# Early final norms of a two-layer encoder trunk: both whole-row passes moved into one turn, statistics one step later, the root four steps into that turn, the store issued by SP

## The chip, the core and the metric

The kernel runs on one core of a Trainium2 chip. Its engines are TensorE (PE), VectorE (DVE), ScalarE (ACT), GpSimd (POOL) and SyncE (SP); each works through its own list of instructions in order, and the lists meet only at semaphores. The metric is the device time of one execution in microseconds (us). Three executions of the kernel before took 3141.05 to 3145.18 us, median 3143.9.

## The reference, cut to what matters

Two layers. Each has a token mixer (latent attention and windowed attention) and then the block below, on 1168 tokens of width 1024 (1024 prompt frames, 128 sample frames, 16 meta tokens). All in float32.

```python
x = layer_norm(ALPHA * x + einsum('btm,md->btd', mix, w_out), ln1_g, ln1_b)
hid = silu(einsum('btd,df->btf', x, wg)) * einsum('btd,df->btf', x, wu)      # 1024 -> 2816
return layer_norm(ALPHA * x + einsum('btf,fd->btd', hid, wd), ln2_g, ln2_b)  # 2816 -> 1024
```

The change concerns the last line's `layer_norm` (the final norm) for the first 640 tokens.

## The kernel before, in words

The feed-forward block takes most of the time. Its hidden width is cut into 11 pairs of chunks (`PAIRS`), its tokens into two groups: group 0 has 640 tokens (five tiles of 128), group 1 has 528. A **turn** is one pair for one group, so a layer has 22 turns, numbered 0 to 21; turns 11 to 21 are group 1's. In this document an even turn means 12, 14, 16, 18 or 20, and an odd turn 13, 15, 17, 19 or 21.

A turn is written as 14 **steps** on every engine. At step i PE computes one product (`product`, 12 matmuls; the weights are multiplied in a scheme with seven products for a two by two block, and each float32 factor is cut into a high and a low part, which makes three matmuls of one). `DOWN_STEPS` places the 16 down products of the turn before (`down`, numbered u = 0 to 15 here, 6 matmuls each) behind steps 2 to 13: u = 4 behind step 5, u = 13 and 14 behind step 12, u = 15 behind step 13. The down products share two PSUM banks, so PE waits before product u until DVE has added product u - 2 to the accumulator `acc` (semaphore `f_y`, helper `down_add`).

The other engines follow. ACT rounds weights to their high part (`woph`, `wdh`); POOL computes the low part (`wopl`, `wdl`; called splits below): one split of `wopl` at each step, and two of `wdl` behind it at steps 1 and 9. DVE combines products (`product_sum`: into `sum_u`, `upper` and `gate`), adds the down products, and forms differences of weights (`T`). The splits of POOL and the `gate`, `T` and `y_early` operations of DVE read two operands from SBUF.

The sum of group 0 is complete when turn 11 ends. Its final norm is therefore done early, one tile of 128 tokens in every two turns, while group 1 is computed. `y_turn_of` names the tile of an even turn (12 to 20: tiles 0 to 4), `y_end_of` that of the odd turn behind it. PE turns the tile (`y_turn`, 8 transposes in the even turn behind u = 5), ACT moves it back into `acc` (`y_move`), and then come the passes that the change moves: `y_stats` (two `bn_stats`, one `bn_aggr`, a small add), `ln_root` on POOL (the power -0.5 of one column), `y_scale` (subtract the mean, times the gain; 128x1024) and `y_norm` (times the root, plus the offset; 128x1024) on DVE, and the store of the rows `y_early` to `H`. `y_early` is one buffer, so `y_scale` waits until the tile before has been stored.

In an even turn, DVE has `y_stats` at step 6 and `y_scale` at step 11, and POOL has `ln_root` at step 9. In the odd turn, DVE has `y_norm` at step 3 and POOL issues the store at step 9. SP issues the loads of the weights; in a turn that is `gate_load`, `down_load`, `up_load`, `down_load`, each behind a wait on POOL's splits (helper `turn`, a loop of the hardware for turns 12 to 20).

Of the kernel before, what the change touches and what calls it, by code (L numbers as in the profile page):

```python
# [13 lines left out]
P = 128  # L14
L = 2
# [18 lines left out]
TILES = 10  # L34
# [14 lines left out]
PAIRS = FC // 2  # L49
# [42 lines left out]
def rows(t):  # L92
    return META if t == TILES - 1 else P


def cols(t):
    return slice(t * P, t * P + rows(t))
# [192 lines left out]
def program(nc, X, LNP, ROT, W_IN, QKVG, W_UQ, W_UK, W_UV, SINKS, MIXG, W_OUT, LN1, W_FF,  # L290
# [7 lines left out]
    with ExitStack() as ctx:  # L298
        names = {}

        def S(name):
            if name not in names:
                names[name] = ctx.enter_context(nc.semaphore(name))
            return names[name]
# [539 lines left out]

        def yo_done(l, t):
            s = t % 4
            return 16 * ((TILES // 2 if s < 2 else 0) + len(range(s, TILES, 4)) * l + t // 4 + 1)

        def small_loads(l, which):

# [225 lines left out]
        def _(sp):  # L1076
            for l in range(L):
# [22 lines left out]
                if l >= 1:  # L1100

                    sp.wait_ge(S("ln_norm"), norms_done(l - 1, EARLY_TILES - 1))
                    for i in range(2):
                        sp.wait_ge(S(f"yo_out{i}"), yo_done(l - 1, i))
                first_loads()
                for t in range(2, TILES):
                    sp.wait_ge(S("a_xT"), A(l, t - 2) + 1)
                    if l == 0:
                        sp.wait_ge(S(f"yo_out{t % 2}"), 16 * (t // 2))
                    else:  # L1110
                        sp.wait_ge(S(f"yo_out{t % 4}"), yo_done(l - 1, t))
                    tile_load(t)
                    sp.wait_ge(S("a_rope"), A(l, t - 2) + 1)
                    sp.dma_start(rot[t % 2][0:rows(t), :], ROT[cols(t), :]).then_inc(S(f"rot_in{t % 2}"), 16)
                    if t == 3:
                        load_split(sp, l, "B", slice(0, 2))
                    if t >= 6:
                        load_split(sp, l, "B", slice(t - 4, t - 3))
# [125 lines left out]
                def residual_load(s):  # L1244
                    t = row_tile(s)
                    if s >= 1:
                        sp.wait_ge(S("n1_out"), 16 * (9 * l + s))
                    sp.dma_start(hc[0:rows(t), :], H[l, cols(t), :]).then_inc(S("hc_in"), 16)

                def x_load(g):  # L1250
                    for i, t in enumerate(X_GROUPS[g]):
# [103 lines left out]
                turn(0, c, False)  # L1355
                sp.wait_ge(S("f_prod"), PRODUCTS * (TURNS * l + PAIRS))
                load_params(sp, l, "D")
                with sp.Fori(1, PAIRS - 1) as j:
                    turn(j, c, False)
                turn(PAIRS - 1, c, True)  # L1360
                sp.wait_ge(S("f_prod"), PRODUCTS * TURNS * (l + 1))
                if l + 1 < L:
                    for k in (2, 0, 1):
                        w_in_load(sp, l + 1, k)
            barrier(sp, phase_no(L - 1, "D"))


# [14 lines left out]
        def _(pool):  # L1382
# [14 lines left out]
            for l in range(L):  # L1397
# [137 lines left out]
                def turn(j, c, no=None):  # L1535
                    downs, ahead = no != 0, no != TURNS - 1
                    for i in range(PRODUCTS):
                        if i < 7 or ahead:
                            w_lo(j, c, i + 7, no == 0 and i == 13)
                        if no == PAIRS - 1 and i in (12, 13):  # L1540
                            x_op_lo(i - 12)
                        if no == PAIRS and i == 1:
                            x_op_lo(5)
                        if i == 1 and downs:
                            down_lo(j - 1, c, 1)
                        if i == (13 if no in (0, PAIRS - 1) else 9):
                            down_lo(j, c, 0)
                        if i == 9 and y_turn_of(no) is not None:
                            ln_root(pool, qD(l, y_turn_of(no)), P)
                        if i == 9 and y_end_of(no) is not None:  # L1550
                            y = y_end_of(no)
                            pool.wait_ge(S("ln_out"), qD(l, y) + 1)
                            pool.dma_start(H[l + 1, cols(y), :], y_early[:, :]).then_inc(S(f"yo_out{y % 4}"), 16)

                c = TURNS * l
                for i in range(2):
# [554 lines left out]
        def _(dve):  # L2111
# [13 lines left out]
            for l in range(L):  # L2125
# [409 lines left out]
                def residual(s):  # L2535
                    r, q = rows(row_tile(s)), A(l, s)
                    dve.wait_ge(S("c_y"), q + 1)
                    dve.wait_ge(S("hc_in"), 16 * (q + 1))
                    dve.scalar_tensor_tensor(out=hc[0:r, :], in0=hc[0:r, :], scalar=ALPHA, in1=YB[0:r, :],
                                             op0=ALU.mult, op1=ALU.add).then_inc(S("c_res"), 1)  # L2540
                    dve.wait_ge(S("c_res"), q + 1)
                    ln_stats(dve, qC(l, s), hc, r)
# [166 lines left out]
                    else:  # L2709
                        dve.tensor_tensor(a, a, down_bank(u, g), ALU.add).then_inc(S("f_y"), 1)  # L2710

                def y_stats(t):

                    q = qD(l, t)
                    dve.wait_ge(S("f_moved"), y_moved(l, t, 1))
                    dve.wait_ge(S("ln_out"), q - 3)
                    for half in range(2):
                        ins = dve.bn_stats(stats[q % 2][:, 6 * half:6 * half + 6], y_rows(t, half))
                    ins.then_inc(S("ln_parts"), 1)
                    dve.wait_ge(S("ln_parts"), 2 * q + 1)  # L2720
                    dve.bn_aggr(mv[ln_slot(q)][:, :], stats[q % 2][:, :]).then_inc(S("ln_parts"), 1)
                    dve.wait_ge(S("ln_parts"), 2 * q + 2)
                    dve.tensor_scalar(veps[ln_slot(q)][:, :], mv[ln_slot(q)][:, 1:2], LN_EPS, None, ALU.add)\
                       .then_inc(S("ln_eps"), 1)

                def y_scale(t):

                    q = qD(l, t)
                    if t:
                        dve.wait_ge(S(f"yo_out{(t - 1) % 4}"), yo_done(l, t - 1))  # L2730
                    else:
                        params(dve, (l, "D"))
                    dve.scalar_tensor_tensor(out=y_early[:, :].rearrange("p (k n) -> p k n", n=P), in0=y_rows(t),
                                             scalar=mv[ln_slot(q)][:, 0:1],
                                             in1=lnd[:, 0:D].rearrange("p (k n) -> p k n", n=P),
                                             op0=ALU.subtract, op1=ALU.mult).then_inc(S("ln_norm"), 1)
# [9 lines left out]
                def turn(j, c, g, no=None):  # L2746

                    first, last, scaled = no == 0, no == TURNS - 1, no in (1, PAIRS + 1)
                    before = 0 if no == PAIRS else g
                    for i in range(PRODUCTS):  # L2750
                        if i == 0 and not first:
                            hid_lo(j - 1, c, before)
                        if i % 7:
                            product_sum(j, c, g, i, first)
                        if no == PAIRS and i in (0, 2):
                            x_op_lo(1, 4 + i)
                        for u in range(DOWNS):
                            if DOWN_STEPS[u] == i and not first:
                                down_add(j - 1, c, before, u, scaled)
                        if i == 1:  # L2760
                            w_sum(j, c, 1, 1)
                            w_sum(j, c, 1, 2)
                        if i in (3, 4):
                            w_sum(j, c, 1, i)
                        if no == PAIRS - 1 and i in (7, 8, 9, 10):
                            x_sum(1, (3, 2, 4, 6)[i - 7])
                        if i == 8 and not last:
                            w_sum(j, c, 2, 1, second=first)
                            w_sum(j, c, 2, 2, second=first)
                        if i in (9, 10) and not last:  # L2770
                            w_sum(j, c, 2, i - 6, second=first)
                        if first and i == 13:
                            x_in9()
                        if i == 3 and y_end_of(no) is not None:
                            y_norm(y_end_of(no))
                        if i == 6 and y_turn_of(no) is not None:
                            y_stats(y_turn_of(no))
                        if i == 11 and y_turn_of(no) is not None:
                            y_scale(y_turn_of(no))
                        if first and i == 3:  # L2780
                            first_norm(9)
                        if no == PAIRS - 1 and i in (11, 12):
                            x_op_lo(1, i - 9)
# [763 lines left out]
```

## Time and profile before

| | us |
|---|---|
| median of three executions | 3143.9 (3141.05 to 3145.18) |
| the profiled execution | 3138.92 |
| its span, first to last instruction | 3137.1 |
| around the span | 1.82 |
| PE busy | 2920.8 (93%) |
| DVE busy | 2162.6 (69%) |
| POOL busy | 1739.7 (55%) |
| ACT busy | 1248.7 (40%) |

The page of the profile gives shares over the whole span, and the stages differ: it says that PE works most of the time, but not which engine PE waits for in the turns that the change touches. That is read from the stretch of turns 12 to 21, which lies at 1208 to 1548 us in layer 0 and at 2761 to 3101 us in layer 1, turn by turn.

### The profile page before, as it was taken

The numbers are of one execution on the slowest core, as the hardware profiler recorded it, in microseconds if no ns is written. First come the engines' busy times: TensorE is split into PE (matmuls) and PEld (weight loads), VectorE is DVE, ScalarE is ACT, GpSimd is POOL, SyncE is SP. The second block draws the span as 40 slices with busy tenths as digits, with TensorE's granted clock in tenths as the row PEclk, the third lists the DMA queues.
The fourth block names the chain that finished last, engine by engine and source line by source line (L and its number), as shares of the span: only waits on it lengthen the run. The fifth ranks groups of instructions, "written<-read, shape, count | busy, mean of one in ns | idle before, by whom it ended". The sixth has DMA issues, their size and how long they took to land. (4 is left out here: it accounts for less than half of the span.)

```text
span 3137.1 us, 56230 instructions
## 1 busy us (share of the span) xinstructions
PE 2920.8 (93%) x20464; PEld 2653.7 (85%) x20464; DVE 2162.6 (69%) x3887; ACT 1248.7 (40%) x2432; POOL 1739.7 (55%) x1348
## 2 busy tenths in 40 slices
PE   7979998999999999999989699989999999999997
PEld 6956666887999999999989566668889999999997
DVE  6757776667666677777755577766576666877776
ACT  3324334435333344444333334444453333444442
POOL 2323332436766668787632233434276666787875
PEclk9989997999999999999989899979999999999999
DMA  4321114543222213333322211156432222233231
GB/s 171 126 83 50 42 39 149 161 159 115 87 83 82 81 57 118 102 101 104 126 90 96 83 41 41 35 162 182 147 116 81 80 80 80 68 111 112 95 102 55
DMA packets 175873, 305.65 MB, mean 97 GB/s; under 512 B 56080, under 2 KB 97296, under 8 KB 175344
## 3 DMA queue, kind: packets, MB, share of 16 engines
q1 hardware_dynamic: 165088, 271.70, 27.0%
q0 software_dynamic: 10576, 31.14, 2.5%
q8 instruction: 135, 2.21, 0.3%
q14 instruction: 74, 0.61, 0.1%
HBM read 248.34 MB, written 50.38 MB: 95 GB/s over the span
## 5 line engine op out<-in xcount | busy, mean ns | idle before, releaser
L2843 PE MATMUL PS<-xoh,woph 128*128 128x320 f32 (+1 forms) x2464 | 735.7, 299 | 14.4 <-issue 11.3
L2845 PE MATMUL PS<-xoh,wopl 128*128 128x320 f32 (+1 forms) x2464 | 733.2, 298 | 0.0
L2844 PE MATMUL PS<-xol,woph 128*128 128x320 f32 (+1 forms) x2464 | 732.0, 297 | 0.0
L1519 POOL TENSOR_TENSOR wopl<-T,woph 128x512 fp32r<-128x512 f32 x348 | 536.3, 1560 | 138.5 <-ACT woph L1988 138.4
L2843 PEld LDWEIGHTS PS<-xoh,woph 128*128 128x128 f32 x2464 | 466.1, 189 | 18.2 <-issue 13.3
L2844 PEld LDWEIGHTS PS<-xol,woph 128*128 128x128 f32 x2464 | 466.2, 189 | 0.2
L2845 PEld LDWEIGHTS PS<-xoh,wopl 128*128 128x128 f32 x2464 | 465.9, 189 | 0.0
L2843 PE MATMUL PS<-hidh,wdh 128*128 128x320 f32 (+1 forms) x1408 | 420.5, 299 | 26.2 <-DVE acc L2710 20.6
L1466 POOL TENSOR_TENSOR Pl<-Pf,Ph 128x256 fp32r<-128x256 f32 (+5 forms) x174 | 219.0, 1265 | 391.0 <-DVE Ph L2390 391.0
L1988 ACT ACTIVATE woph<-T 128x512 fp32r<-128x512 f32 x348 | 216.8, 630 | 515.5 <-DVE T L2652 293.7
L2845 PE MATMUL PS<-hidh,wdl 128*128 128x320 f32 (+1 forms) x1408 | 417.5, 297 | 0.0
L2844 PE MATMUL PS<-hidl,wdh 128*128 128x320 f32 (+1 forms) x1408 | 416.7, 296 | 0.0
L2710 DVE TENSOR_TENSOR acc<-acc,PS 128x320 f32<-128x320 f32 (+1 forms) x608 | 273.6, 454 | 142.1 <-PE PS L2845 141.6
L2843 PEld LDWEIGHTS PS<-hidh,wdh 128*128 128x128 f32 x1408 | 264.5, 188 | 34.4 <-DVE acc L2710 27.7
L1526 POOL TENSOR_TENSOR wdl<-rd,wdh 128x512 fp32r<-128x512 f32 x176 | 265.9, 1530 | 29.8 <-ACT wdh L1997 29.8
L1519 POOL TENSOR_TENSOR wopl<-rg,woph 128x512 fp32r<-128x512 f32 x128 | 184.1, 1440 | 154.3 <-ACT woph L1988 154.3
L2845 PEld LDWEIGHTS PS<-hidh,wdl 128*128 128x128 f32 x1408 | 264.5, 188 | 0.0
L2844 PEld LDWEIGHTS PS<-hidl,wdh 128*128 128x128 f32 x1408 | 264.4, 188 | 0.0
L1519 POOL TENSOR_TENSOR wopl<-ru,woph 128x512 fp32r<-128x512 f32 x132 | 192.7, 1469 | 104.1 <-ACT woph L1988 103.1
L1793 ACT ACTIVATE Pf<-PS 128x512 f32<-128x512 f32 (+5 forms) x174 | 127.8, 752 | 284.7 <-PE PS L2952 284.1
L2843 PE MATMUL PS<-winh,xTh 128*128 128x394 f32 (+3 forms) x480 | 170.3, 355 | 9.7 <-DVE xTl L2137 5.6
L2696 DVE TENSOR_TENSOR upper<-PS,sum_u 128x264 f32<-128x264 f32 (+1 forms) x176 | 80.9, 460 | 124.6 <-PE PS L2845 121.9
(487 smaller groups left out, 6655.9 us busy)
## 6 DMA issues: line engine op xcount, KB each, us to landing
ru<-in_W_FF SPq DMA_DIRECT2D x88, 512.0 KB, 4.1
rd<-in_W_FF SPq DMA_DIRECT2D x176, 256.0 KB, 2.7
rg<-in_W_FF SPq DMA_DIRECT2D x82, 512.0 KB, 4.2
sqt_scratch<-sqTs POOLq DMA_DIRECT2D x18, 512.0 KB, 4.0
hc<-out_H SPq DMA_DIRECT2D x18, 512.0 KB, 3.6
dkraw<-in_CKVT SPq DMA_DIRECT2D x16, 520.0 KB, 4.4
QS<-sqt_scratch SPq DMA_DIRECT2D x16, 512.0 KB, 3.4
mt<-mix_scratch SPq DMA_DIRECT2D x16, 512.0 KB, 4.6
```

The costliest lines, as they stand in the source:

```text
L1466: ins = pool.tensor_tensor(Pl[i][0:kk, 1, c], Pf[i][0:kk, 1, c], f(Ph[i][0:kk, 1, c]), ALU.subtract)
L1519: pool.tensor_tensor(wopl[k][:, :, :], w_whole(w, k, first), f(woph[k][:, :, :]), ALU.subtract)\
L1526: pool.tensor_tensor(wdl[:, n, e, :], rd[n][:, :, :], f(wdh[:, n, e, :]), ALU.subtract)\
L1793: ins = act.activation(Pf[r][0:kk, :, c], both_banks(u)[0:kk, :, c], ACT.Exp)
L1988: act.activation(woph[k][:, :, :], w_whole(w, k, first or second), ACT.Copy).then_inc(S("f_hi"), 1)
L2696: dve.tensor_tensor(up, product, rest, ALU.add).then_inc(S("f_made"), 1)
L2710: dve.tensor_tensor(a, a, down_bank(u, g), ALU.add).then_inc(S("f_y"), 1)
L2843: pe.matmul(out, wh, mh, start=start, stop=False)
L2844: pe.matmul(out, wh, ml, start=False, stop=False)
L2845: return pe.matmul(out, wl, mh, start=False, stop=stop)
```

## The change

Statistics: `y_stats` goes from step 6 to step 7 of the even turn and keeps only the two `bn_stats`; the aggregate and the small add become `y_mean` at step 11 of the even turn, where `y_scale` stood. `y_scale` goes to step 6 and `y_norm` to step 11 of the odd turn. `ln_root` goes to step 4 of the odd turn. The store is issued by SP at the end of its odd turn, behind a wait for `y_norm`; SP's loop is written out for that, and the store counts on the semaphore `hrow`, which the loads of `hc` share.

```diff
@@ SP
-                with sp.Fori(1, PAIRS - 1) as j:
-                    turn(j, c, False)
-                turn(PAIRS - 1, c, True)
+                def y_store(t):
+                    sp.wait_ge(S("ln_out"), qD(l, t) + 1)
+                    sp.dma_start(H[l + 1, cols(t), :], y_early[:, :]).then_inc(S("hrow"), 16)
+
+                for j in range(1, PAIRS):
+                    turn(j, c, j == PAIRS - 1)
+                    if y_end_of(PAIRS + j) is not None:
+                        y_store(y_end_of(PAIRS + j))
...
@@ SP, start of layer 1
-                    for i in range(2):
-                        sp.wait_ge(S(f"yo_out{i}"), yo_done(l - 1, i))
+                    sp.wait_ge(S("hrow"), y_stored(l - 1, EARLY_TILES - 1))
...
@@ POOL, turn
-                        if i == 9 and y_turn_of(no) is not None:
-                            ln_root(pool, qD(l, y_turn_of(no)), P)
-                        if i == 9 and y_end_of(no) is not None:
-                            y = y_end_of(no)
-                            pool.wait_ge(S("ln_out"), qD(l, y) + 1)
-                            pool.dma_start(H[l + 1, cols(y), :], y_early[:, :]).then_inc(S(f"yo_out{y % 4}"), 16)
+                        if i == 4 and y_end_of(no) is not None:
+                            ln_root(pool, qD(l, y_end_of(no)), P)
...
@@ DVE, turn
-                        if i == 3 and y_end_of(no) is not None:
+                        if i == 7 and y_turn_of(no) is not None:
+                            for half in range(2):
+                                y_stats(y_turn_of(no), half)
+                        if i == 11 and y_turn_of(no) is not None:
+                            y_mean(y_turn_of(no))
+                        if i == 6 and y_end_of(no) is not None:
+                            y_scale(y_end_of(no))
+                        if i == 11 and y_end_of(no) is not None:
                             y_norm(y_end_of(no))
-                        if i == 6 and y_turn_of(no) is not None:
-                            y_stats(y_turn_of(no))
-                        if i == 11 and y_turn_of(no) is not None:
-                            y_scale(y_turn_of(no))
```

How the rows of the engines move is shown at three places. The first is DVE at the end of an even turn, steps 11 and 12. Before, the scaling pass stands ahead of step 12's `upper` and `gate`:

```order
L2679 TENSOR_TENSOR sum_u_311<-PS,sum_u_312 128x264
L2707 SCALAR_TENSOR_TENSOR acc_324<-acc_324,PS 128x264
L2733 SCALAR_TENSOR_TENSOR y_early<-acc_297,mv_349,lnd 128x1024
L2696 TENSOR_TENSOR upper<-PS,sum_u_311 128x264
L2699 TENSOR_TENSOR gate<-upper,gate 128x264
L2707 SCALAR_TENSOR_TENSOR acc_324<-acc_324,PS 128x264 x2
```

With the change, two small operations on the statistics stand in its place:

```order
L2685 TENSOR_TENSOR sum_u_311<-PS,sum_u_312 128x264
L2713 SCALAR_TENSOR_TENSOR acc_324<-acc_324,PS 128x264
L2731 BN_AGGR mv_349<-stats_54 128x2
L2733 TENSOR_SCALAR veps_353<-mv_349 128x1
L2702 TENSOR_TENSOR upper<-PS,sum_u_311 128x264
L2705 TENSOR_TENSOR gate<-upper,gate 128x264
```

The pass of 1024 columns has left the row ahead of the two additions u = 13 and 14.

The second place is DVE in an odd turn. Before, the second pass stands at step 3, ahead of step 4's two sums and the addition u = 2:

```order
L2652 TENSOR_TENSOR T_330<-ru_329 128x512
L2743 SCALAR_TENSOR_TENSOR y_early<-y_early,rstd_357,lnd 128x1024
L2693 TENSOR_TENSOR gate<-PS,sum_u_313 128x264
L2679 TENSOR_TENSOR sum_u_311<-PS,sum_u_312 128x264
L2710 TENSOR_TENSOR acc_324<-acc_324,PS 128x264
```

With the change, this turn has the first pass at step 6, between the additions u = 5 and u = 6, and further on the second pass at step 11, behind the addition u = 12:

```order
L2716 TENSOR_TENSOR acc_324<-acc_324,PS 128x264
L2743 SCALAR_TENSOR_TENSOR y_early<-acc_297,mv_349,lnd 128x1024
...
L2685 TENSOR_TENSOR sum_u_311<-PS,sum_u_312 128x264
L2753 SCALAR_TENSOR_TENSOR y_early<-y_early,rstd_357,lnd 128x1024
L2702 TENSOR_TENSOR upper<-PS,sum_u_311 128x264
L2705 TENSOR_TENSOR gate<-upper,gate 128x264
```

Steps 3 and 4 are rid of a pass, and the end of the odd turn has taken one.

The third place is POOL in an odd turn, from step 9 on. Before, the store is issued between the splits of the down weights and those of steps 10 to 12:

```order
L1526 TENSOR_TENSOR wdl<-rd_327,wdh 128x512
L1553 DMA out_H<-y_early 128x1024
L1519 TENSOR_TENSOR wopl_305<-T_322,woph_304 128x512
L1519 TENSOR_TENSOR wopl_326<-T_330,woph_325 128x512
L1519 TENSOR_TENSOR wopl_319<-T_331,woph_318 128x512
```

With the change, the splits follow each other, and the root stands earlier in the turn, behind step 4's split:

```order
L1529 TENSOR_TENSOR wopl_326<-T_330,woph_325 128x512
L713 TENSOR_TENSOR rstd_357<-veps_353,half 128x1
L1529 TENSOR_TENSOR wopl_319<-T_331,woph_318 128x512
...
L1536 TENSOR_TENSOR wdl<-rd_327,wdh 128x512
L1529 TENSOR_TENSOR wopl_305<-T_322,woph_304 128x512
```

In the even turn the root goes out of the same place, between the down splits and step 10's.

## Rows read from the trace of the kernel before

**Rows 1.** Windows: turns 12 and 13 of layer 0 (length, busy time and count, PE clock).

```profile
1208.02:1242.13 34.11, 33.36 (x274) 32.91 (x274) 26.64 (x50) 14.91 (x28) 27.46 (x20) 1.00 0.28 93
1242.13:1276.22 34.09, 32.56 (x267) 32.14 (x266) 26.85 (x46) 13.82 (x26) 28.07 (x20) 1.00 0.32 109
```

**Rows 2.** Groups by line, PE, turns 12 to 20 of layer 0: down products, idle before them.

```profile
L2843 PE MATMUL PS<-hidh,wdh 128*128 128x264 f32 x288 | 83.0, 288 | 9.4 <-DVE acc L2710 8.8 <-DVE acc L2707 0.7
```

**Rows 3.** Timeline, PE: start, duration, operation, idle before it, at u = 15, 4, 15.

```profile
1240.33 0.29 PE L2845 MATMUL PS<-xoh,wopl 128*128 128x264 f32 x1
1241.28 0.39 PE L2843 MATMUL PS<-hidh,wdh 128*128 128x264 f32 x1 [0.66 <-DVE acc L2707]
1241.50 0.29 PE L2844 MATMUL PS<-hidl,wdh 128*128 128x264 f32 x1
1241.63 0.29 PE L2845 MATMUL PS<-hidh,wdl 128*128 128x264 f32 x1
...
1253.63 0.28 PE L2845 MATMUL PS<-hidh,wdl 128*128 128x264 f32 x1
1254.60 0.39 PE L2843 MATMUL PS<-hidh,wdh 128*128 128x264 f32 x1 [0.69 <-DVE acc L2710]
...
1274.25 0.29 PE L2845 MATMUL PS<-xoh,wopl 128*128 128x264 f32 x1
1275.37 0.39 PE L2843 MATMUL PS<-hidh,wdh 128*128 128x264 f32 x1 [0.84 <-DVE acc L2710]
```

**Rows 4.** Timeline, DVE, end of turn 12: steps 11 and 12.

```profile
1236.04 0.65 DVE L2699 TENSOR_TENSOR gate<-upper,gate 128x264 f32<-128x264 f32 x1
...
1237.29 2.15 DVE L2733 SCALAR_TENSOR_TENSOR y_early<-acc,mv,lnd 128x1024 f32<-128x1024 f32 x1
1239.37 0.42 DVE L2696 TENSOR_TENSOR upper<-PS,sum_u 128x264 f32<-128x264 f32 x1
1239.82 1.06 DVE L2699 TENSOR_TENSOR gate<-upper,gate 128x264 f32<-128x264 f32 x1
1240.81 0.42 DVE L2707 SCALAR_TENSOR_TENSOR acc<-acc,PS 128x264 f32<-128x264 f32 x1
```

**Rows 5.** Timeline, POOL, end of turn 12: the root and step 10's split.

```profile
1236.35 0.74 POOL L713 TENSOR_TENSOR rstd<-veps,half 128x1 f32<-128x1 f32 x1
1237.06 1.31 POOL L1519 TENSOR_TENSOR wopl<-T,woph 128x512 fp32r<-128x512 f32 x1
```

**Rows 6.** Timeline, DVE, turn 13: the second pass, the additions u = 2 and u = 6.

```profile
1251.21 2.32 DVE L2743 SCALAR_TENSOR_TENSOR y_early<-y_early,rstd,lnd 128x1024 f32<-128x1024 f32 x1
...
1254.13 0.41 DVE L2710 TENSOR_TENSOR acc<-acc,PS 128x264 f32<-128x264 f32 x1
...
1260.03 0.43 DVE L2710 TENSOR_TENSOR acc<-acc,PS 128x264 f32<-128x264 f32 x1 [1.78 <-PE PS L2845]
```

**Rows 7.** Timeline, DVE, end of turn 13: step 12 and the addition u = 13.

```profile
1271.67 0.43 DVE L2696 TENSOR_TENSOR upper<-PS,sum_u 128x264 f32<-128x264 f32 x1 [0.38 <-PE PS L2845]
1272.14 2.84 DVE L2699 TENSOR_TENSOR gate<-upper,gate 128x264 f32<-128x264 f32 x1
1274.90 0.42 DVE L2710 TENSOR_TENSOR acc<-acc,PS 128x264 f32<-128x264 f32 x1
```

**Rows 8.** Timeline, POOL, end of turn 13: the store's issue, the splits of steps 10 to 12.

```profile
1270.26 0.62 POOL L1553 DMA_DIRECT2D out_H<-y_early  x1
1270.90 1.30 POOL L1519 TENSOR_TENSOR wopl<-T,woph 128x512 fp32r<-128x512 f32 x1
...
1272.15 2.52 POOL L1519 TENSOR_TENSOR wopl<-T,woph 128x512 fp32r<-128x512 f32 x2
```

**Rows 9.** Timeline, DVE, turn 12, steps 6 to 8.

```profile
1224.57 1.29 DVE L2718 BATCH_NORM_STATS2 stats<-acc 128x6 f32<-128x512 f32 x2 [1.38 <-ACT acc L2018]
1225.89 0.21 DVE L2721 BATCH_NORM_AGGREGATE mv<-stats 128x2 f32<-128x12 f32 x1
...
1226.21 0.42 DVE L2707 SCALAR_TENSOR_TENSOR acc<-acc,PS 128x264 f32<-128x264 f32 x1
...
1227.56 0.43 DVE L2696 TENSOR_TENSOR upper<-PS,sum_u 128x264 f32<-128x264 f32 x1 [0.93 <-PE PS L2845]
```

**Rows 10.** Timeline, SP's queue, end of turn 13: loads issued.

```profile
1270.48 0.33 SPq L1320 DMA_DIRECT2D rd<-in_W_FF  x1
1276.72 0.86 SPq L1295 DMA_DIRECT2D rg<-in_W_FF  x2
```

More of the change, by code:

```diff
@@ L846, in yo_done, with y_stored @@
             s = t % 4
-            return 16 * ((TILES // 2 if s < 2 else 0) + len(range(s, TILES, 4)) * l + t // 4 + 1)
+            late = range(EARLY_TILES, TILES)
+            return 16 * ((TILES // 2 if s < 2 else 0) + sum(i % 4 == s for i in late) * l + sum(i % 4 == s for i in late if i <= t))
+        def y_stored(l, t):
+            return 16 * (TILES * (l + 1) + EARLY_TILES * l + t + 1)
         def small_loads(l, which):
@@ L1109, in _ @@
                         sp.wait_ge(S(f"yo_out{t % 2}"), 16 * (t // 2))
-                    else:
+                    elif t >= EARLY_TILES:
                         sp.wait_ge(S(f"yo_out{t % 4}"), yo_done(l - 1, t))
@@ L1247, in residual_load @@
                         sp.wait_ge(S("n1_out"), 16 * (9 * l + s))
-                    sp.dma_start(hc[0:rows(t), :], H[l, cols(t), :]).then_inc(S("hc_in"), 16)
+                    sp.dma_start(hc[0:rows(t), :], H[l, cols(t), :]).then_inc(S("hrow"), 16)
                 def x_load(g):
@@ L1364, in _ @@
                         w_in_load(sp, l + 1, k)
+            sp.wait_ge(S("hrow"), y_stored(L - 1, EARLY_TILES - 1))
             barrier(sp, phase_no(L - 1, "D"))
@@ L2537, in residual @@
                     dve.wait_ge(S("c_y"), q + 1)
-                    dve.wait_ge(S("hc_in"), 16 * (q + 1))
+                    dve.wait_ge(S("hrow"), 16 * (q + EARLY_TILES * l + 1))
                     dve.scalar_tensor_tensor(out=hc[0:r, :], in0=hc[0:r, :], scalar=ALPHA, in1=YB[0:r, :],
@@ L2710, in down_add, with y_stats, y_mean @@
                         dve.tensor_tensor(a, a, down_bank(u, g), ALU.add).then_inc(S("f_y"), 1)
-                def y_stats(t):
+                def y_stats(t, half):
                     q = qD(l, t)
-                    dve.wait_ge(S("f_moved"), y_moved(l, t, 1))
+                    dve.wait_ge(S("f_moved"), y_moved(l, t, half))
                     dve.wait_ge(S("ln_out"), q - 3)
-                    for half in range(2):
-                        ins = dve.bn_stats(stats[q % 2][:, 6 * half:6 * half + 6], y_rows(t, half))
-                    ins.then_inc(S("ln_parts"), 1)
+                    ins = dve.bn_stats(stats[q % 2][:, 6 * half:6 * half + 6], y_rows(t, half))
+                    if half:
+                        ins.then_inc(S("ln_parts"), 1)
+                def y_mean(t):
+                    q = qD(l, t)
                     dve.wait_ge(S("ln_parts"), 2 * q + 1)
@@ L2729, in y_scale @@
                     if t:
-                        dve.wait_ge(S(f"yo_out{(t - 1) % 4}"), yo_done(l, t - 1))
+                        dve.wait_ge(S("hrow"), y_stored(l, t - 1))
                     else:
```

## The prediction

> **What bounds the kernel now.** I read the windows of two neighbouring turns first, then what PE waits for in the turns, then each wait on the timelines. In the windows of turns 12 and 13 [rows 1] both turns take 34.1 us, PE is busy for 32.6 to 33.4 us of each, and its clock is granted in full. DVE works 26.6 and 26.9 us and POOL 27.5 and 28.1 us, so neither is full: PE sets the pace, and what can be won is PE's idle time. The group view over turns 12 to 20 gives it one cause: 9.4 us ahead of the first matmuls of down products, ended by DVE's additions into `acc` [rows 2].
>
> The timeline shows where. Within a product PE starts a matmul every 0.12 to 0.13 us (1241.50 to 1241.63). Three times in two turns it doesn't [rows 3]:
> - end of the even turn, u = 15: 1240.33 to 1241.28, so 0.83 us beyond the pace, and the next interval is 0.22 us (0.10 more): **0.93 us**;
> - odd turn, u = 4: 1253.63 to 1254.60: 0.85 + 0.10 = **0.95 us**;
> - end of the odd turn, u = 15: 1274.25 to 1275.37: 1.00 + 0.10 = **1.10 us**.
>
> I take the restart of the first for the other two. These three are all: the view counts 0.66, 0.69 and 0.84 us of idle time for them, and five even ends, four u = 4 and four odd ends in turns 12 to 20 make 3.3 + 2.8 + 3.4 = 9.4 us, the sum of [rows 2]. Both layers have ten even turns and ten odd ones; turn 21, the last of a layer, has POOL without splits at its end, and I count no odd end for it. So the most that this change can win there is 10 x 0.93 + 10 x 0.95 + 8 x 1.10 = 27.6 us.
>
> Each wait ends with an addition on DVE, and the row of DVE says what made it late:
> - Even end: u = 15 needs u = 13's addition, which runs at 1240.81. Ahead of it stand `y_scale`, 2.15 us from 1237.29, then `upper`, then a `gate` of 1.06 us [rows 4].
> - u = 4 needs u = 2's addition at 1254.13, behind `y_norm`, 2.32 us from 1251.21 [rows 6].
> - Odd end: no norm stands there. One `gate` takes 2.84 us from 1272.14 [rows 7] while POOL runs three splits back to back, 1270.90 to 1274.67 [rows 8].
>
> **A DVE operation with two SBUF operands waits for POOL's split.** `y_scale` asks at 1237.29, POOL's split runs from 1237.06 to 1238.37 [rows 5], and 1.07 us after its end `y_scale` is done. So about half of each norm pass is waiting for POOL, and where the pass lies in POOL's row matters as much as where it lies in DVE's.
>
> **The change, part by part.** The sum is made against the profiled execution: 3138.92 us, a span of 3137.1 with 1.82 around it, 5.0 below the median of the three runs (3143.9). I subtract the gain from the median.
>
> *Pass out of the odd turn's step 3.* u = 2's addition comes 2.3 us earlier, PE needs 0.85: the wait goes, 0.95 us. *First pass into step 6.* DVE idles 1.78 us ahead of u = 6's addition at 1260.03 [rows 6], so the pass starts at 1258.25. It costs 1.1 us alone, and at most one split of 1.3 us more before it, so it ends by 1260.7 and pushes u = 6 by at most 0.6 us. PE needs that addition at u = 8: behind u = 6, as product 8 and u = 7, 18 matmuls, 2.2 us, come first. Hidden; without that cover it would cost 0.6 us a turn. Gain **0.95 x 10 = 9.5 us**.
>
> *Even end.* `y_mean` takes `y_scale`'s place: from 1225.89 to 1226.21 the same two operations hold DVE for 0.32 us [rows 9]. `upper` then starts when product 12 is done. In turn 13 that was 1271.67, 2.70 us ahead of where u = 15 would have started unhindered (1274.25 + 0.12); in turn 12 it is 1240.45 - 2.70 = 1237.75. `gate` asks 0.47 us later, at 1238.22. POOL has lost its root (1236.35 to 1237.06 [rows 5]), so its first split starts at 1236.35, is held by step 11's `gate` until some 1236.6 (that `gate` ends at 1236.69 [rows 4]), and ends near 1237.87. The second runs to 1239.13. `gate` gets in behind it, takes some 0.3 us (in turn 13 from POOL's end at 1274.67 to 1274.98), and u = 13 is added by 1239.8, 0.6 us before PE wants it. The wait goes: **0.93 x 10 = 9.3 us**. Its other bound is 0.1 us: if `gate` is held through two splits, as in turn 13, it is done at 1240.7, u = 13 at 1241.1, and u = 15 starts only 0.1 us earlier than now.
>
> *Statistics at step 7.* They start behind u = 6's addition, near 1226.45, and end at 1227.75, 0.2 us past the time at which `upper` begins now, where DVE idled 0.93 us [rows 9]. The `T` differences and POOL's row follow 0.2 us later, which leaves 0.4 of the 0.6 us above. Nothing for PE.
>
> *Odd end.* The store leaves POOL's row (0.62 us at 1270.26 [rows 8]), the second pass enters DVE's. This is the even end as it stands now, with one difference: no root ahead of the splits. The first split ends some 0.47 us earlier relative to PE than at 1238.37 (0.70 of the root, less 0.25 for which `gate` holds it). So the wait is 0.83 - 0.47 + 0.10 = 0.46 in place of 1.10 us. Gain **0.64 x 8 = 5.1 us**; bounds: all of 1.10, or none. In turn 21 the pass waits for no split and fits.
>
> *Root and store.* The root at step 4 adds at most 0.74 us to a row of POOL's that needs nothing from PE for seven steps (`wopl` of step i feeds product i + 7). On SP the store stands between the `rd` loads at 1270.48 and the `rg` loads at 1276.72 [rows 10]; `y_norm` ends near 1273, so no load waits. Were it some 4 us later, `rg` would wait, and those operands are wanted only from the next turn's step 7. At the end of layer 0 the tile loads wait for the last store, and PE wants them after the late norms. Nothing.
>
> Sum: 9.5 + 9.3 + 5.1 = **23.9 us**. 3138.9 becomes 3115.0, and the median of 3143.9 becomes **3120.0**.
>
> The Trainium skill ("SBUF — State Buffer", "SBUF: two separate sides") says that DVE operations with two SBUF inputs and GpSimd's operations share one port pair under an exclusive lock, and that whoever starts first has it for its whole instruction. The 2.84 us `gate` differs: it starts at 1272.14, the split behind it at 1272.15, and yet two splits pass first. By the page's rule `gate` at the even end waits for one split, and the sum is the one above.
>
> **Rivals.**
> 1. *The row of splits keeps the ends late.* As in turn 13, `gate` loses to two splits at the even end (gain 0.1 us), and at the odd end the pass costs what the store's 0.62 us gives back (gain 0). For it: the 2.84 us, which comes without any norm pass near it. Against it: in the odd turns `gate` asks within 0.02 us of a split's start, here 0.2 to 0.35 us behind one, like `y_scale` (0.23 us behind), which lost to one split. Only u = 4 is won: 9.5 + 1.0 = 10.5 us, 3133.4.
> 2. *All waits go*, as DVE at the odd end gets in earlier than I reckon: 27.6 us, 3116.3.
> 3. *The other side: `y_norm` loses the port at the odd end to the whole row of three splits.* It asks near 1271.29, where DVE goes idle now [rows 7]; the row ends near 1274.3; the pass ends at 1275.4, `upper`, `gate` and u = 13 at 1276.7, and PE starts u = 15 at 1276.8 in place of 1274.37. That is 2.4 us, 0.4 more than u = 4 and the odd end lose now; with the even end's `gate` held by the same row nothing else is won. With 8 x 0.4 us lost, 2 x 0.95 won in the two turns 21 and 1.0 at the even ends, three splits come out even; a fourth costs 1.3 x 8 = 10 us, and from there on the kernel is slower: 3154. For it: two splits in a row have passed a waiting DVE. Against it: only at coinciding starts, and the row has three splits before POOL waits for ACT.
> 4. *Nothing moves*: each wait removed is met by DVE's next addition at the same place. Against it: the idle times ahead of the additions at u = 5 and u = 6. 3143.
>
> **How the numbers follow.** Forecast 0.55, rival 1 0.22, rival 2 0.11, rival 3 0.05, rival 4 0.07. The median is uncertain by 2 us either way, so a change of 0.2%, 6.3 us, is what can be told from none. Rivals 1 and 2 are faster by more: 0.88 in all; 0.08 the same, with rival 4 and a weaker rival 3; 0.04 slower. The range is from 3114, rival 2 less 2 us, to 3135, rival 1 plus 2 us.
>
> **What would show it.** Right: no PE idle time ahead of u = 4 in odd turns; none at even ends, and DVE's `gate` there well below 1.5 us; about 0.4 us at odd ends; turns of 33.2 and 32.6 us. Wrong: a `gate` of 2 us or more at step 12 of either turn, an addition u = 6 or later that PE waits for, or `y_norm` above 2.5 us.

## The result, and the profile after

The changed kernel took 3112.79 to 3115.55 us in four runs, median 3114.23; the kernel before, run beside it, had a median of 3142.48. The ratio is 0.992, 95% interval 0.9902 to 0.9939: faster by 0.8%, where 3120.0 us (3114 to 3135) was forecast against 3143.9, a ratio of 0.9924. The profiled execution took 3112.79 us, 26.1 less than that of before.

The windows of turns 12 and 13 answer to [rows 1] (length, then busy time and count of PE, weight loads, DVE, ACT and POOL, PE clock, DMA share, GB/s):

```profile
1206.09:1239.30 33.21, 33.12 (x275) 32.88 (x274) 24.84 (x49) 14.81 (x28) 25.95 (x18) 1.00 0.30 98
1239.30:1271.74 32.44, 32.29 (x267) 32.08 (x265) 26.89 (x47) 13.80 (x27) 27.46 (x20) 1.00 0.33 115
```

33.2 and 32.4 us were 34.1 each, at the same full clock. PE's busy time is down by 0.24 and 0.27 us (a matmul that restarts after a wait is recorded 0.1 us longer), so most of the gain is idle time. The group view of turns 12 to 20 says where from: PE's idle time ahead of the first matmuls of down products was 9.4 us [rows 2] and is 0.6.

```profile
L2856 PE MATMUL PS<-hidh,wdh 128*128 128x264 f32 x288 | 82.0, 285 | 0.6
```

The timeline of PE at the three places of [rows 3] (start, duration, operation):

```profile
1238.43 0.29 PE L2858 MATMUL PS<-xoh,wopl 128*128 128x264 f32 x1
1238.56 0.28 PE L2856 MATMUL PS<-hidh,wdh 128*128 128x264 f32 x1
...
1250.81 0.29 PE L2858 MATMUL PS<-hidh,wdl 128*128 128x264 f32 x1
1250.93 0.28 PE L2856 MATMUL PS<-hidh,wdh 128*128 128x264 f32 x1
...
1270.47 0.29 PE L2858 MATMUL PS<-xoh,wopl 128*128 128x264 f32 x1
1270.91 0.39 PE L2856 MATMUL PS<-hidh,wdh 128*128 128x264 f32 x1
1271.13 0.28 PE L2857 MATMUL PS<-hidl,wdh 128*128 128x264 f32 x1
```

u = 15 of the even turn and u = 4 follow at the pace of 0.12 to 0.13 us; only the odd end still waits: 0.44 and 0.22 us, 0.42 beyond the pace. DVE's timeline at the end of turn 12 answers to [rows 4], those of turn 13 to [rows 6, 7]:

```profile
1235.47 0.20 DVE L2731 BATCH_NORM_AGGREGATE mv<-stats 128x2 f32<-128x12 f32 x1
1235.70 0.15 DVE L2733 TENSOR_SCALAR veps<-mv 128x1 f32<-128x1 f32 x1
1235.86 0.43 DVE L2702 TENSOR_TENSOR upper<-PS,sum_u 128x264 f32<-128x264 f32 x1
1236.33 1.23 DVE L2705 TENSOR_TENSOR gate<-upper,gate 128x264 f32<-128x264 f32 x1
1237.48 0.76 DVE L2713 SCALAR_TENSOR_TENSOR acc<-acc,PS 128x264 f32<-128x264 f32 x2
...
1254.39 2.30 DVE L2743 SCALAR_TENSOR_TENSOR y_early<-acc,mv,lnd 128x1024 f32<-128x1024 f32 x1
1256.62 0.42 DVE L2716 TENSOR_TENSOR acc<-acc,PS 128x264 f32<-128x264 f32 x1
...
1267.44 1.64 DVE L2753 SCALAR_TENSOR_TENSOR y_early<-y_early,rstd,lnd 128x1024 f32<-128x1024 f32 x1
1269.00 0.42 DVE L2702 TENSOR_TENSOR upper<-PS,sum_u 128x264 f32<-128x264 f32 x1
1269.45 1.06 DVE L2705 TENSOR_TENSOR gate<-upper,gate 128x264 f32<-128x264 f32 x1
```

`y_mean` takes the place of the pass at the even end, and `gate` there lasts 1.23 us. The first pass takes 2.30 us at step 6, the second 1.64 at step 11. `gate` at the odd end takes 1.06 us where it took 2.84, although a pass now stands ahead of it.

Not all of the 26.1 us is the change. Turn 0 of a layer, which the change doesn't touch, took 50.41 us in both layers before and 48.82 and 49.01 after, 3.0 us of the 26.1. The changed kernel profiled once more (e11 below) had that of layer 0 at 50.41; windows of turn 0, first and second profile:

```profile
725.30:774.12 48.82, 43.45 (x257) 39.05 (x255) 41.57 (x51) 24.44 (x39) 38.08 (x22) 0.97 0.34 122
```

```profile
730.90:781.31 50.41, 43.45 (x258) 39.01 (x256) 41.60 (x51) 24.54 (x39) 38.10 (x22) 0.97 0.35 118
```

In the 14 profiles of this study a turn 0 took 48.8 to 49.0 us 9 times and 50.1 to 50.5 us 19 times, in one layer or the other whatever the kernel. So the experiments are read from the turns, which repeat to some hundredths of a microsecond. The stretch, from PE's first matmul of turn 12 to the first of the layer's last down products, went from 342.4 and 342.3 us (the two layers) to 330.1 and 330.0: the change is worth **24.5 us** (the two differences, before they are rounded).

### The profile page after: what moved, and what is told of

Same layout as the page of the kernel before. It is cut to its first block and busy times, and to the rows that moved or that the text cites. A ratio compares the mean times of both kernels' runs of the same rounds, so it can differ in the third digit from the quotient of the medians.

```text
span 3111.0 us, 55804 instructions
## 1 busy us (share of the span) xinstructions
PE 2919.6 (94%) x20464; PEld 2655.7 (85%) x20464; DVE 2158.1 (69%) x3887; ACT 1246.5 (40%) x2432; POOL 1719.2 (55%) x1338
## 3 DMA queue, kind: packets, MB, share of 16 engines
q1 hardware_dynamic: 166528, 276.94, 27.6%
## 5 line engine op out<-in xcount | busy, mean ns | idle before, releaser
L2858 PE MATMUL PS<-xoh,wopl 128*128 128x320 f32 (+1 forms) x2464 | 732.4, 297 | 0.0
L1529 POOL TENSOR_TENSOR wopl<-T,woph 128x512 fp32r<-128x512 f32 x348 | 525.8, 1528 | 144.2 <-ACT woph L1994 144.2
L2857 PE MATMUL PS<-winl,xTh 128*128 128x394 f32 (+3 forms) x480 | 166.8, 347 | 0.0
```

The lines of the kernel that those rows point to most:

```text
L1529: pool.tensor_tensor(wopl[k][:, :, :], w_whole(w, k, first), f(woph[k][:, :, :]), ALU.subtract)\
L2857: pe.matmul(out, wh, ml, start=False, stop=False)
L2858: return pe.matmul(out, wl, mh, start=False, stop=stop)
```

## The experiments

Turns are means over turns 12 to 20 of both layers, the stretch is that of layer 0; the ratio is to the kernel before, run beside each.

| kernel | even turn | odd turn | stretch | ratio (95%) |
|---|---|---|---|---|
| before | 34.12 | 34.09 | 342.4 | |
| changed | 33.18 | 32.44 | 330.1 | 0.992 (0.9902-0.9939) |
| e1 `y_norm` at step 6 | 34.12 | 33.15 | 337.6 | 0.9962 (0.9943-0.9981) |
| e2 as e1, root at step 4 | 33.59 | 33.14 | 334.8 | 0.994 (0.992-0.996) |
| e3 store on SP alone | 34.09 | 32.99 | 337.8 | 0.9968 (0.9958-0.9979) |
| e4 changed, `y_norm` at step 8 | 33.18 | 32.04 | 328.4 | 0.991 (0.9894-0.9927) |
| e5 before, `gate` asks later | 34.12 | 34.09 | 342.3 | 1.0013 (1.0004-1.0023) |
| e6 changed, old statistics and root | 33.18 | 32.44 | 330.1 | 0.9932 (0.9915-0.9948) |
| e8 as e4, store on POOL | 33.19 | 33.49 | 334.3 | 0.9954 (0.994-0.9969) |
| e9 as e4, power on POOL | 33.18 | 32.04 | 328.5 | 0.9906 (0.989-0.9921) |
| e10 as e1, store at step 8 | 34.12 | 32.06 | 333.2 | 0.9955 (0.9939-0.9971) |
| e11 changed again | 33.19 | 32.44 | 330.1 | 0.9939 (0.9925-0.9954) |
| e12 as e4 again | 33.18 | 32.04 | 328.4 | 0.9924 (0.9911-0.9937) |
| e13 as e4, one row stored by POOL | 33.19 | 33.44 | 334.1 | 0.9986 (0.9974-0.9999) |

**e1, the pass alone.**

```diff
-                        if i == 3 and y_end_of(no) is not None:
+                        if i == 6 and y_end_of(no) is not None:
                             y_norm(y_end_of(no))
```

> Kernel before with one edit: y_norm goes from step 3 to step 6 of the odd turn. Statistics, y_scale, root and store stay where they were. My theory: only the wait ahead of u = 4 goes (0.95 us, ten times in two layers), because the pass at step 6 lies in DVE idle time; the ends of the turns keep their waits of 0.93 and 1.10 us. The stretch from turn 12 to the last down products, 342.3 us in each layer before, becomes 337.5; the whole run is 9.5 us shorter. Rival, nothing moves: the pass pushes u = 6 to u = 8 and PE waits there; the stretch stays above 340.

Odd turns got 0.94 us shorter, turn 21 0.95, even turns nothing: the wait at u = 4 and no other.

**e2, and the root.**

```diff
-                        if i == 9 and y_turn_of(no) is not None:
-                            ln_root(pool, qD(l, y_turn_of(no)), P)
+                        if i == 4 and y_end_of(no) is not None:
+                            ln_root(pool, qD(l, y_end_of(no)), P)
```

> As the kernel with y_norm at step 6, and the root goes from step 9 of the even turn to step 4 of the odd turn; the pass y_scale stays at step 11 of the even turn. My theory: without the root POOL's splits start 0.47 us earlier, so y_scale gets the port 0.47 us earlier and the even end's wait falls from 0.93 to 0.46 us: 4.7 us in ten turns, the stretch 335.2 us per layer. Rival: the splits' row settles around the pass as before, whatever stands ahead of it: 337.5.

Even turns got 0.54 us shorter than in e1: the root ahead of the splits does delay the pass, by about the 0.47 us reckoned.

**e3, the store alone.** DVE and the root as before, SP's store, its counts and waits as in the change.

```diff
-                        if i == 9 and y_end_of(no) is not None:
-                            y = y_end_of(no)
-                            pool.wait_ge(S("ln_out"), qD(l, y) + 1)
-                            pool.dma_start(H[l + 1, cols(y), :], y_early[:, :]).then_inc(S(f"yo_out{y % 4}"), 16)
...
+                    if y_end_of(PAIRS + j) is not None:
+                        y_store(y_end_of(PAIRS + j))
```

> Kernel before with one edit: the store is issued by SP at the end of the odd turn; passes, statistics and root at their old steps. Question: why did the odd end's gate lose to two splits. Theory A (ties alone lose twice): without the 0.62 us issue the row of splits starts 0.62 us earlier, gate asks in the middle of the second split, waits for that one alone, and the odd end's wait of 1.10 us goes: 8.8 us in eight turns, the stretch 337.9 us per layer instead of 342.3. Theory B (a row of splits back to back is passed as a whole): gate waits until the third split ends, 0.62 us earlier than before: 5.0 us, 339.8 per layer. Theory C: the issue was not on the path, 342.3.

The odd turn got 1.10 us shorter, by all of the odd end's wait. Timeline of POOL and DVE there (the first row is three splits back to back):

```profile
1272.42 4.18 POOL L1529 TENSOR_TENSOR wopl<-T,woph 128x512 fp32r<-128x512 f32 x3
1274.29 1.16 DVE L2705 TENSOR_TENSOR gate<-upper,gate 128x264 f32<-128x264 f32 x1
```

`gate` asks in the second split and is done 1.16 us later, before the third has run. That fitted theory A, that only coinciding starts lose twice.

**e4, the second pass at step 8.**

```diff
-                        if i == 11 and y_end_of(no) is not None:
+                        if i == 8 and y_end_of(no) is not None:
                             y_norm(y_end_of(no))
```

> Changed kernel with one edit: y_norm at step 8 of the odd turn instead of step 11. My theory: the odd end keeps no pass, its wait of 0.41 us goes in eight turns, and step 8 hides the pass: the stretch from turn 12 to the last down products, 330.0 to 330.1 us per layer in the changed kernel, becomes 328.4; the run 3.3 us shorter. Rival 1: the pass makes PE wait for the additions behind step 8: 330 or more. Rival 2: with no pass and no store near it the end's gate meets the start of a split again and is passed by two, as in [rows 7]: a gate of 2.8 us and 332 or more.

The odd turn got another 0.40 us shorter, as my theory said. The pass takes 1.28 us at step 8, where POOL waits for ACT; `gate` asks 0.06 us behind the second split's start and is passed by that one alone (1.53 us), which PE doesn't notice. Timeline of POOL (the second split) and DVE at the end of turn 13:

```profile
1267.05 1.29 POOL L1529 TENSOR_TENSOR wopl<-T,woph 128x512 fp32r<-128x512 f32 x1
...
1267.11 1.53 DVE L2705 TENSOR_TENSOR gate<-upper,gate 128x264 f32<-128x264 f32 x1
```

**e5, the coincidence put to the test.**

```diff
                     dve.wait_ge(S("f_acted"), acted(j, c, "g" + QUARTERS[x]))
+                    if x == 2 and isinstance(j, int) and y_end_of(j) is not None:
+                        dve.tensor_scalar(veps[0][:, :], mv[0][:, 1:2], LN_EPS, None, ALU.add)
                     dve.tensor_tensor(out, up, out, ALU.mult).then_inc(S("f_made"), 1)
```

> Kernel before with work added and nothing moved: in the odd turns one tensor_scalar on a 128x1 column that nobody reads, between upper and gate at step 12, so that gate asks for the port some 0.15 us later. In [rows 7, 8] gate asks at 1272.14 and a split starts at 1272.15; in the kernel with the store on SP gate asks 0.42 us behind a split's start and in the one with y_norm at step 8 0.06 us behind it, and each time one split passes. Theory A (only a request within some hundredths of a split's start is passed by two): gate falls from 2.84 to about 1.5 us, the odd end's wait of 1.10 us goes, odd turns take 33.0 us instead of 34.1, the stretch 337.9 us instead of 342.3: more work, a shorter run. Theory B (a row back to back passes as a whole, the other two kernels differ for another reason): gate ends where it did, the turns stay at 34.1.

A miss: the turns did not change (the run as a whole was 0.1% longer, which no turn from 12 on shows). Timeline of POOL and DVE at the end of turn 13, the second split once more by itself:

```profile
1274.23 0.62 POOL L1553 DMA_DIRECT2D out_H<-y_early  x1
...
1274.87 3.77 POOL L1519 TENSOR_TENSOR wopl<-T,woph 128x512 fp32r<-128x512 f32 x3
...
1276.12 0.15 DVE L2700 TENSOR_SCALAR veps<-mv 128x1 f32<-128x1 f32 x1
...
1276.12 1.29 POOL L1519 TENSOR_TENSOR wopl<-T,woph 128x512 fp32r<-128x512 f32 x1
...
1276.19 2.75 DVE L2701 TENSOR_TENSOR gate<-upper,gate 128x264 f32<-128x264 f32 x1
```

`gate` asks 0.07 us behind the second split's start, as in e4 (0.06), and is passed by two where it was passed by one there. The moment of the request within a split is out. What differs is the row of POOL: an issue stands ahead of it here, and its three splits take 3.77 us together; without the issue they take 4.18, because DVE gets in between.

**e6, statistics and root back.** Both `bn_stats` and `y_mean` at step 6, the root at step 9 of the even turn, the rest as changed.

```diff
-                        if i == 4 and y_end_of(no) is not None:
-                            ln_root(pool, qD(l, y_end_of(no)), P)
+                        if i == 9 and y_turn_of(no) is not None:
+                            ln_root(pool, qD(l, y_turn_of(no)), P)
...
-                        if i == 7 and y_turn_of(no) is not None:
+                        if i == 6 and y_turn_of(no) is not None:
                             for half in range(2):
                                 y_stats(y_turn_of(no), half)
-                        if i == 11 and y_turn_of(no) is not None:
                             y_mean(y_turn_of(no))
```

> Changed kernel with statistics (both bn_stats, aggregate, small add) back at step 6 and the root back at step 9 of the even turn; passes and store as changed. My theory: nothing in the turns, 33.2 and 32.4 us, the stretch 330.1 us: with the pass away, a gate behind a split that starts 0.47 us later still adds u = 13 before PE wants it. Rival: the root's 0.7 us shows at the even end as it did beside y_scale: even turns 33.7, the stretch 332.7.

No difference in any turn. The root, worth 0.54 us beside the pass, is worth nothing once the pass is gone.

**e8, the store back on POOL.** The kernel of e4 with POOL's issue at step 9 of the odd turn, as it stood before; SP's store, its counts and SP's written-out loop go back as well and are left out here.

```diff
+                        if i == 9 and y_end_of(no) is not None:
+                            y = y_end_of(no)
+                            pool.wait_ge(S("ln_out"), qD(l, y) + 1)
+                            pool.dma_start(H[l + 1, cols(y), :], y_early[:, :]).then_inc(S(f"yo_out{y % 4}"), 16)
```

> Kernel with y_norm at step 8 of the odd turn, but the store issued by POOL at step 9 of the odd turn as before. It tells whether the store had to leave POOL. Theory A (only the moment of the request counts): the issue puts the splits 0.62 us later, gate asks 0.9 us into the first of them instead of 0.06 us into the second, is passed by one, and PE waits for nothing: odd turns 32.04 us as with the store on SP, the stretch 328.5. Theory B (0.62 us on POOL ahead of the splits is 0.62 us at the end of the turn): odd turns 32.4 us or more, 330 or more.

Theory B, and by far more than its 0.62 us: the odd turn got 1.45 us longer than in e4. Timeline of POOL and DVE:

```profile
1268.55 0.62 POOL L1553 DMA_DIRECT2D out_H<-y_early  x1
...
1269.19 3.78 POOL L1519 TENSOR_TENSOR wopl<-T,woph 128x512 fp32r<-128x512 f32 x3
...
1270.07 3.20 DVE L2699 TENSOR_TENSOR gate<-upper,gate 128x264 f32<-128x264 f32 x1
...
1273.20 1.28 POOL L1519 TENSOR_TENSOR wopl<-rg,woph 128x512 fp32r<-128x512 f32 x1 [0.23 <-ACT woph L1988]
```

`gate` asks in the first split, 0.88 us behind its start, and all three pass, up to the place where POOL waits for ACT. If the issue did no more than put the splits later by its length, `gate` should have waited for one; e9 tries that.

**e9, the issue or its length.** In the kernel of e4, an operation of about the issue's length in its place (its result is not read).

```diff
+                        if i == 9 and y_end_of(no) is not None:
+                            pool.tensor_tensor(rstd[0][:, :], half[:, :], half[:, :], ALU.pow)
```

> Kernel with y_norm at step 8 and the store on SP, and at step 9 of the odd turns, where POOL issued the store in the kernel before, one more power on a 128x1 column that nobody reads (0.55 to 0.77 us). With the store's issue there PE waited 1.36 us at the odd end and the gate took 3.20 us, passed by every split up to POOL's next pause; a request 0.07 us behind a split's start, moved by an added operation, was passed by two as well, so the coincidence of starts is out. Theory D (it is the DMA issue ahead of them that lets a row of splits pass): an operation as long in its place puts the splits at the same time, and gate is passed by one split only: gate below 1.5 us, odd turns 32.04 us, the stretch 328.5. Theory P (it is the time at which the splits run): gate near 3.2 us, odd turns 33.5 us.

Timeline of POOL and DVE:

```profile
1269.09 0.74 POOL L1561 TENSOR_TENSOR rstd<-half 128x1 f32<-128x1 f32 x1
...
1269.80 3.99 POOL L1529 TENSOR_TENSOR wopl<-T,woph 128x512 fp32r<-128x512 f32 x3
...
1270.60 0.79 DVE L2707 TENSOR_TENSOR gate<-upper,gate 128x264 f32<-128x264 f32 x1
```

The splits run as late as behind the issue, `gate` asks 0.80 us into the first (0.88 in e8), and one passes: 0.79 in place of 3.20 us. Theory D holds: what counts is the issue and not the time that it takes.

**e10, a pause behind the issue.** In the kernel of e1:

```diff
-                        if i == 9 and y_end_of(no) is not None:
+                        if i == 8 and y_end_of(no) is not None:
                             y = y_end_of(no)
                             pool.wait_ge(S("ln_out"), qD(l, y) + 1)
```

> Kernel with y_norm at step 6 of the odd turn and all else as before, and the store is issued by POOL at step 8 of the odd turn instead of step 9. Behind it POOL still waits 1.5 us for ACT before its next split. Theory D2 (an issue lets the splits pass that follow it without a pause): the pause separates them, gate at step 12 of the odd turn is passed by one split, below 1.5 us, and the odd end's wait of 1.1 us goes: odd turns 32.05 us instead of 33.15, even turns stay at 34.1, the stretch 333.1 instead of 337.5. Theory D3 (the issue marks POOL until something else ends it, pause or not): gate 2.8 us, odd turns 33.15.

Timeline of POOL and DVE, the issue and then the end of the turn:

```profile
1255.78 0.62 POOL L1553 DMA_DIRECT2D out_H<-y_early  x1
1258.03 1.62 POOL L1519 TENSOR_TENSOR wopl<-T,woph 128x512 fp32r<-128x512 f32 x1 [1.62 <-ACT woph L1988]
1259.62 3.00 POOL L1526 TENSOR_TENSOR wdl<-rd,wdh 128x512 fp32r<-128x512 f32 x2
...
1260.67 0.78 DVE L2652 TENSOR_TENSOR T<-rg,T 128x512 f32<-128x512 f32 x1
...
1262.57 4.19 POOL L1519 TENSOR_TENSOR wopl<-T,woph 128x512 fp32r<-128x512 f32 x3
...
1264.43 1.17 DVE L2699 TENSOR_TENSOR gate<-upper,gate 128x264 f32<-128x264 f32 x1
```

POOL still issues the store, one step earlier, and the odd end has no wait: 32.06 us for 33.15, as theory D2 forecast. That it is the pause is not shown, though: between the issue and the row lie the pause of 1.62 us, three other splits, and 6.2 us in all. In e8 DVE got in 3.8 us after the issue's end, when the row was over. Here the first of its operations with two SBUF operands to ask during a split, `T` at 1260.67, got in between two splits, 4.5 us after the issue's end. So something that lasts some 4 us behind an issue would fit as well as something that ends with a pause.

**e11 and e12, side by side.** The changed kernel and that of e4 once more.

> The changed kernel once more, to stand on the same chip beside the one with y_norm at step 8: 3.3 us longer than that, 0.1%. Turn 0 of a layer takes 48.8 or 50.4 us by chance in the kernels so far, whatever their change.

> The kernel with y_norm at step 8 once more: stretch 328.5 us in both layers, 3.3 us shorter than the changed kernel in the whole run.

The stretches repeat to 0.1 us: 330.1 and 328.4. The medians were 3121.36 and 3113.61 us; of these 7.8 us the turns explain 3.3, the rest is the spread outside them (turn 0, and the mixing stage between the layers). So the kernel with `y_norm` at step 8 is the better one by its turns, by 0.1%; e9 has the same turns.

**e13, the issue or its transfer.** In the kernel of e4, POOL stores row 0 of the tile, SP the other 127; the waits and counts that follow from it are left out here.

```diff
-                    sp.dma_start(H[l + 1, cols(t), :], y_early[:, :]).then_inc(S("hrow"), 16)
+                    sp.dma_start(H[l + 1, P * t + 1:P * t + P, :], y_early[1:P, :]).then_inc(S("hrow"), 16)
...
+                        if i == 9 and y_end_of(no) is not None:
+                            pool.dma_start(H[l + 1, P * y:P * y + 1, :], y_early[0:1, :]).then_inc(S(f"yo_out{y % 4}"), 16)
```

> Kernel with y_norm at step 8 and the store on SP, but the first of the tile's 128 rows (4 KB) is stored by POOL at step 9 of the odd turn, SP stores the other 127. With the whole store issued there (issue at 1268.55 for 0.62 us, landed 4.4 us later by the median) gate waited until 1272.97, which was the end of the row of splits and about the landing as well. Theory I (the issue itself: splits that follow it without a pause pass as a row, whatever its size): gate about 3 us, PE waits 1 us or more, odd turns 33.2 us or more. Theory L (it lasts as long as POOL's transfer is under way): 4 KB land sooner, gate is passed by one split or two, below 2.5 us, odd turns 32.04 to 32.4 us.

Timeline of POOL and DVE:

```profile
1270.13 0.56 POOL L1564 DMA_DIRECT2D out_H<-y_early  x1
...
1270.71 3.79 POOL L1530 TENSOR_TENSOR wopl<-T,woph 128x512 fp32r<-128x512 f32 x3
...
1271.65 3.15 DVE L2710 TENSOR_TENSOR gate<-upper,gate 128x264 f32<-128x264 f32 x1
```

Theory I holds: 4 KB cost what 512 KB cost, and SP's store and loop, which e8 took back, stay here. From issue to landing the 4 KB took 3.0 us by the median (4.4 in e8), and yet DVE got in only 4.4 us after the issue began, at the end of the row. The run as a whole is 0.1% shorter than before and not 0.5% as the stretch would have it, since from layer 0's last down products to turn 0 of layer 1 it took 739.9 us, where the other profiles have 721.8 to 732.4; that I did not follow up.

## Why the prediction was right, and where its reasons were not

- *Pass out of step 3*: 0.95 us a turn forecast, 0.94 and 0.95 measured by itself in e1. At step 6 it pushes u = 6 by 0.37 us (17.32 us into the turn; before 17.90 [rows 1, 6], of which 0.95 was the wait at u = 4), forecast at most 0.6. Hidden, as reckoned. A pass alone takes 1.28 us (e4) where 1.1 was reckoned; nothing hung on it.
- *Even end*: 0.93 forecast, 0.94 measured. The steps hold as well: with the turn's start 1.93 us earlier than in [rows 1], `gate` was forecast to ask at 1236.29 and did at 1236.33. It waits for one split, POOL's second (1235.98 for 1.28 us). This is also what the rule of the Trainium skill gave ("SBUF — State Buffer", "SBUF: two separate sides"), and the 1.23 us agree with it.
- *Statistics, root*: nothing forecast, nothing in e6.
- *Odd end*: a wait of 0.46 us forecast, 0.42 measured; 0.64 us a turn forecast, 0.70 measured (34.09 less 0.95 less 32.44). *The reason failed.* Of the store's move I saw only the 0.62 us of its issue, and I put the 2.84 us of [rows 7] down to coinciding starts. The store's move alone is worth 1.10 us (e3), all of the odd end's wait, because without an issue ahead of them the splits no longer pass as a row (e5, e9); the pass put there costs 0.40 us (e4). That the sum came out is luck as far as the reason goes: I took the odd end from the even end, and there no issue stands ahead of the splits.
- *Store on SP*: nothing forecast for the loads, and none waits for it. It is issued at 1269.10, the `rg` loads follow at 1273.19, behind POOL:

```profile
1264.86 2.04 SPq L1323 DMA_DIRECT2D rd<-in_W_FF  x2
1269.10 0.34 SPq L1364 DMA_DIRECT2D out_H<-y_early  x1
1273.19 0.81 SPq L1298 DMA_DIRECT2D rg<-in_W_FF  x2
```

- *The sum*: 0.94 x 10 + 0.95 x 10 + 0.70 x 8 = 24.5 us for 23.9. Rival 1 had a true core (a row of splits can pass) and the wrong condition; e8 shows what it costs where the condition is met. Rival 2 is what e4 does: 342.4 to 328.4 and 342.3 to 328.5 are 27.8 us for 27.6. Rival 3 did not come: `y_norm` waited for one split, 0.55 us. Nor did rival 4: the three waits did not move to DVE's next addition, the turns are shorter.
- *The median*: 3114.23 us is 5.8 below the forecast and 0.2 inside the range. The two medians differ by 28.3 us, of which the turns explain 24.5; the rest is the spread outside them. e11 had 3121.36 for the same kernel, so the 2 us by which I took the median to be uncertain are too few, and where in the range it fell is chance.

## What to carry to other kernels

Read each wait of the bounding engine by itself, and take the cost of a step that is moved to a new place from a place with the same neighbours on the other engine: that carried this prediction to within 0.6 us over a wrong reason. On POOL, let no row of operations stand directly behind a DMA issue when DVE needs two SBUF operands soon after: issue from SP (e3, e4), or earlier, with a pause of POOL's in between (e10). And when a kernel's stages repeat to hundredths of a microsecond, compare the stages; here the rest of the run moves by several microseconds from one execution to the next.

## What the runs showed of the hardware that I had not expected

A DVE operation with two SBUF operands that asks while POOL's split runs is let in at the end of that split: 0.79 to 1.54 us for `gate` at the odd ends of e3, e4, e9, e10 and e12, and 1.06 in the changed kernel. With a DMA issue of POOL's directly ahead of the row it is let in only at the end of the row, where POOL next waits for ACT: 2.74 to 3.22 us, in every odd turn 13 to 19 of layer 0 in before, e1, e2, e5, e8 and e13, whether it asks 0.07 us (e5) or 0.88 us (e8) into a split, whether 512 KB or 4 KB are stored. A power of 0.74 us in the issue's place doesn't do it (e9), nor does an issue 6.2 us ahead of the row, with a pause and other splits in between (e10). The exclusive lock of the Trainium skill ("SBUF — State Buffer", "SBUF: two separate sides"), held by whoever started first for the whole instruction, accounts for the wait for one split, and there the traces agree with it. It does not say that the next split may pass a DVE operation that waits already; behind an issue one more does (e5), or two (e8). It is not the transfer as such: SP's store of the same rows was under way at these times too (in e12 it was issued at 1269.31, with 3.7 us to landing by the median, and `gate` asked at 1270.37 and took 1.54 us). What the issue leaves behind in POOL stays open, and so does what ends it: every row of splits directly behind an issue was three splits long here, so the end of the row, the pause behind it and 3.8 us from the issue's end (e8, e13) fall together.
